# Two transformer blocks on one core: the convolution's splits moved a unit ahead, the entry and the end in another order

## What is computed

```python
def hybrid_mixer(h, ...):
    z = hp @ w_in
    c_q, c_kv, k_pe, gate_b, gate_c, x_in = jnp.split(z, SPLITS, axis=-1)
    ...
    attn = causal_block_attention(q_nope, q_rope, k_nope, k_rope, v)
    u = gate_c * x_in
    u_pad = jnp.pad(u, ((0, 0), (CONV_W - 1, 0), (0, 0)))
    y = sum(conv_w[k] * u_pad[:, k:k + plen] for k in range(CONV_W))
    conv = gate_b * y
    merged = jnp.concatenate([rms_norm(attn[:, PAD_FRONT:], attn_out_norm),
                              rms_norm(conv[:, PAD_FRONT:], conv_out_norm)], axis=-1)
    return merged @ w_out

def second_block(x, ...):
    ...
    h = h + (jax.nn.silu(u @ w_ffn_gate[l]) * (u @ w_ffn_up[l])) @ w_ffn_down[l]
    return rms_norm_2(h, norm_final)
```

## Time and profile before

| | |
|---|---|
| runs shown | 690.18, 691.2, 689.23 us |
| the profiled execution | 689.03 us |
| its span on the core | 687.2 us, so 1.83 us lie around it |
| PE busy | 640.4 us (93%) |
| DVE, ACT, POOL busy | 351.2, 290.0, 51.7 us |
| transferred | 180.73 MB, mean 263 GB/s |

### The profile page before, as it was taken

The page is one execution under the profiler, slowest core; times in us unless marked ns, Lnnn a source line. Parts: engine busy times, 40 slices in busy tenths (PEclk is TensorE's granted clock), DMA queues, the critical chain, the costliest instruction groups (busy, mean ns, idle before and its releaser), DMA issues.

```text
span 687.2 us, 10211 instructions
## 1 busy us (share of the span) xinstructions
PE 640.4 (93%) x4037; PEld 483.7 (70%) x4037; DVE 351.2 (51%) x678; ACT 290.0 (42%) x552; POOL 51.7 (8%) x76
## 2 busy tenths in 40 slices
PE   8999899999999776879899999999999999999995
PEld 5979888842543320424399999998788888888884
DVE  4687664731031020110187766657856666666665
ACT  5855562421011010100182755563665555544554
POOL 3100101100010000000049000000000000000001
PEclk9999999999999997799999999999999999999999
DMA  8956338999999999999997333345535555554101
GB/s 344 419 194 260 116 138 331 403 372 426 427 374 425 420 422 421 422 420 421 422 421 280 123 124 123 123 167 187 185 137 188 189 195 202 198 193 184 62 1 61
DMA packets 26286, 180.73 MB, mean 263 GB/s; under 512 B 3184, under 2 KB 3312, under 8 KB 5120
## 3 DMA queue, kind: packets, MB, share of 16 engines
q1 hardware_dynamic: 25488, 177.89, 65.4%
q10 hardware_dynamic: 752, 2.21, 0.8%
HBM read 179.04 MB, written 1.05 MB: 262 GB/s over the span
## 4 chain that ended last, share of the span: by engine, by line
PE 76%; DMA 11%; DVE 6%; ACT 4%; issue 2%; POOLq 0%; SPq 0%; POOL 0%; ACTq 0%; DVEq 0%
PE ps L1567 73%; DMA ring<-stream_dram 11%; PE ps L1570 3%; DVE ring_r L406 1%; ACT single L399 1%; DVE work L1502 1%; ACT work L850 1%; DVE work L1505 1%; ACT work L757 0%; DVE h L1555 0%; ACT turned L855 0%; ACT work_r L846 0%; DVE work L1388 0%; DVE single L1399 0%; ACT work L764 0%
## 5 line engine op out<-in xcount | busy, mean ns | idle before, releaser
L1567 PE MATMUL ps<-turned,single 128*128 128x256 f32 (+2 forms) x944 | 231.1, 326 | 1.6 <-ACT work L627 0.8
L1567 PE MATMUL ps<-turned,ring_r 128*128 128x256 f32 (+1 forms) x648 | 179.9, 281 | 0.0
L1567 PEld LDWEIGHTS ps<-turned,single 128*128 128x128 f32 x944 | 156.3, 189 | 18.4 <-issue 2.0
L406 DVE TENSOR_TENSOR ring_r<-ring,single 128x1024 fp32r<-128x1024 f32 (+1 forms) x132 | 160.8, 1240 | 14.7 <-ACT single L399 14.7
L399 ACT ACTIVATE single<-ring 128x1024 fp32r<-128x1024 f32 (+1 forms) x132 | 133.8, 1047 | 0.0
L1567 PEld LDWEIGHTS ps<-turned,ring_r 128*128 128x128 f32 x648 | 121.2, 189 | 0.4
L1567 PE MATMUL ps<-ring,work 128*32 128x512 f32 (+2 forms) x462 | 69.8, 612 | 14.7 <-DMA ring<-stream_dram 12.6
L1567 PEld LDWEIGHTS ps<-single 128*128 128x128 f32 x257 | 40.7, 199 | 34.8 <-issue 22.4
L1567 PE MATMUL ps<-work 128*128 128x128 f32 (+5 forms) x310 | 60.5, 378 | 2.6 <-DVE work L1046 1.8
L1567 PE MATMUL ps<-single,turned 128*128 128x512 f32 (+3 forms) x208 | 59.7, 367 | 1.9 <-DVE turned L1187 1.5
L1567 PE MATMUL ps<-single 128*128 128x512 f32 (+1 forms) x257 | 58.0, 367 | 2.9 <-DVE single L1399 1.9
(11 more groups left out here) (254 smaller groups left out, 697.4 us busy)
## 6 DMA issues: line engine op xcount, KB each, us to landing
ring<-stream_dram SPq DMA_DIRECT2D x145, 1024.0 KB, 12.0
work<-stream_dram SPq DMA_DIRECT2D x12, 1024.0 KB, 12.3
turned_w<-stream_dram SPq DMA_DIRECT2D x4, 1024.0 KB, 14.1
extra<-stream_dram SPq DMA_DIRECT2D x2, 1024.0 KB, 9.4
ring<-stream_dram SPq DMA_DIRECT2D x2, 832.0 KB, 7.2
h<-x_dram SPq DMA_DIRECT2D x2, 512.0 KB, 4.5
gain<-gains_dram ACTq DMA_DIRECT2D x2, 512.0 KB, 8.5
yields<-stream_dram SPq DMA_DIRECT2D x1, 1024.0 KB, 12.5
```

Of the source, the lines that this page charges most:

```text
L406: dve.tensor_tensor(ring_r[:, place, a], ring[:, place, a], w_hi[k % HIGHS][:, a].bitcast(F32), ALU.subtract).then_inc(s["wlo_done"], 1)
L1567: return pe.matmul(o, lhsT, rhs, start=start, stop=stop, **kw)
```

## The change

Four things move. At the entry, `vec[:, 0:V_RB]` is issued from ACT's queue, between the meta tokens and the positions, and no longer from SP's; PE's first wait is for constants, meta tokens and the first half of `x` only (`x_in`, 48), and the wait for `vec` and the positions is left to ACT and DVE (`const_in`, 32); the first idle products are three and no longer four, the second two and no longer four. In block 1's attention ACT makes the high parts of rows 0 to 2 in `beside(6)` and of row 3 in `beside(7)`, and the weights' split 10 goes behind these; DVE makes the low parts of rows 0 to 2 in `beside(7)` and of row 3 in `beside(8)`. At the end ACT sums the last squares ahead of `result(0, 1)`; DVE's quarter has a semaphore of its own (`y_left`), for which SP waits; and ACT itself issues the store of the quarter that it finishes last. Two semaphores of extra slots are merged into `const_in`, which then counts 64.

```diff
@@ slot_ready
             elif n == ASIDE_AT + 1 + AGAIN:
-                eng.wait_ge(x_in, 48)
+                eng.wait_ge(x_in, 64)
             elif ASIDE_END - EXTRA <= n < ASIDE_END:
-                eng.wait_ge(extra_full[n - (ASIDE_END - EXTRA)], 16)
+                eng.wait_ge(const_in, 64)
@@ sync
-            sp.dma_start(cst[:, 0:C_FIRST], consts[:, 0:C_FIRST]).then_inc(const_in, 16)
+            sp.dma_start(cst[:, 0:C_FIRST], consts[:, 0:C_FIRST]).then_inc(x_in, 16)
             sp.dma_start(h[:, 0, :], x[0:P, :]).then_inc(x_in, 16)
             sp.dma_start(h[:, 1, :], x[P:TOK, :]).then_inc(x1_in, 16)
-            sp.dma_start(vec[:, 0:V_RB], small[:, 0:V_RB]).then_inc(const_in, 16)
...
-            for i in range(NT):
-                for n in range(2):
-                    sp.wait_ge(s["y_done"], n + 1 if i == 0 else 2 * NT)
-                    sp.dma_start(out[i * P:(i + 1) * P, n * 512:(n + 1) * 512], xn2[:, i, n * 512:(n + 1) * 512]
-                                 ).then_inc(out_st, 16)
+            for n in range(2):
+                sp.wait_ge(s["y_done"], n + 1)
+                sp.dma_start(out[0:P, n * 512:(n + 1) * 512], xn2[:, 0, n * 512:(n + 1) * 512]).then_inc(out_st, 16)
+            sp.wait_ge(s["y_left"], 1)
+            sp.dma_start(out[P:TOK, 512:D], xn2[:, 1, 512:D]).then_inc(out_st, 16)
@@ scalar
             act.dma_start(meta_raw, meta).then_inc(x_in, 16)
+            act.dma_start(vec[:, 0:V_RB], small[:, 0:V_RB]).then_inc(const_in, 16)
             act.dma_start(pos_i[:], positions).then_inc(const_in, 16)
...
-            act.wait_ge(const_in, 48)
+            act.wait_ge(const_in, 32)
...
+            def conv_high(m):
+                act.activation(mrg_hi[:, CT + m, :], mrg[:, m, :], ACT.Copy,
+                               scale=vec[:, V_GCONV + m:V_GCONV + m + 1]).then_inc(s["mrg_high"], 1)
...
                 if u == 6:
+                    act.wait_ge(s["conv_ps"], 3 * CT)
+                    for m in range(CT - 1):
+                        conv_high(m)
+                if u == 7:
+                    conv_square(3)
+                    conv_high(3)
                     split_high_half(act, 10, 0)
-                if u == 7:
-                    act.wait_ge(s["conv_ps"], 3 * CT)
-                    conv_square(3)
-                    for m in range(CT):
-                        act.activation(mrg_hi[:, CT + m, :], mrg[:, m, :], ACT.Copy,
-                                       scale=vec[:, V_GCONV + m:V_GCONV + m + 1]).then_inc(s["mrg_high"], 1)
...
             result(0, 0)
+            last_squares(1, 1)
             result(0, 1)
-            last_squares(1, 1)
             result(1, 0)
+            act.wait_ge(s["y_done"], NT + 1)
+            act.dma_start(out[P:TOK, 0:512], xn2[:, 1, column_half(0)]).then_inc(out_st, 16)
@@ gpsimd
-            pool.wait_ge(const_in, 48)
+            pool.wait_ge(x_in, 48)
@@ vector
-            dve.wait_ge(const_in, 48)
+            dve.wait_ge(const_in, 32)
...
             dve.wait_ge(s["init"], 1)
+            dve.wait_ge(x_in, 48)
...
+            def conv_low(m):
+                dve.wait_ge(s["mrg_high"], m + 1)
+                dve.scalar_tensor_tensor(mrg_lo[:, CT + m, :], mrg[:, m, :], vec[:, V_GCONV + m:V_GCONV + m + 1],
+                                         mrg_hi[:, CT + m, :].bitcast(F32), ALU.mult, ALU.subtract
+                                         ).then_inc(s["convg_done"], 1)
...
                 if u == 7:
                     conv_gated(3)
+                    for m in range(CT - 1):
+                        conv_low(m)
                 if u == 8:
-                    for m in range(CT):
...
+                    conv_low(3)
...
-            dve.tensor_scalar(xn2[:, 1, a], xn2[:, 1, a], rsf[:, 1:2], None, ALU.mult).then_inc(s["y_done"], 1)
+            dve.tensor_scalar(xn2[:, 1, a], xn2[:, 1, a], rsf[:, 1:2], None, ALU.mult).then_inc(s["y_left"], 1)
@@ tensor
-            idle_products(ps[:, 7, 0:ZA], zt[:, 0, 0:P], zt[:, 0, :], 4)
-            pe.wait_ge(const_in, 48)
-            pe.wait_ge(x_in, 32)
+            idle_products(ps[:, 7, 0:ZA], zt[:, 0, 0:P], zt[:, 0, :], 3)
+            pe.wait_ge(x_in, 48)
...
             pe.wait_ge(s["turn_dve"], 1)
-            idle_products(ps[:, 0, 0:ZA], zt[:, 0, 0:P], zt[:, 0, :], 4)
+            idle_products(ps[:, 0, 0:ZA], zt[:, 0, 0:P], zt[:, 0, :], 2)
```

More of the change, by code:

```diff
@@ L311, in two_blocks @@
         full = [sem(f"slot_full{i}") for i in range(SLOTS)]
-        extra_full = [sem(f"extra_full{i}") for i in range(EXTRA)]
         full2 = [sem(f"slot2_full{i}") for i in range(SLOTS)]
@@ L322, in two_blocks @@
             yp_ps yp_sb s2_ps nm2_done e2_done p2_done pt2_ps pt2_sb o2_ps o2_sb sig_done br_ps br_sb
-            mg_done h3_ps h3_done f_ps fsg_done fh_sum fh_high fh_done facc_ps whi_done wlo_done o2_low yp_low mg_sum mg_high att_low cm_ps cm_sb sqs_done h4_done hg_done y_done""".split()
+            mg_done h3_ps h3_done f_ps fsg_done fh_sum fh_high fh_done facc_ps whi_done wlo_done o2_low yp_low mg_sum mg_high att_low cm_ps cm_sb sqs_done h4_done hg_done y_done y_left""".split()
         s = {n: sem(n) for n in names}
@@ L536, in _ @@
                     if n in aside[10:]:
-                        sp.dma_start(home(n), stream[entry_at(n)]).then_inc(extra_full[n - aside[10]], 16)
+                        sp.dma_start(home(n), stream[entry_at(n)]).then_inc(const_in, 16)
                         continue
@@ L594, in _ @@
             split_high(act, 1)
-            act.wait_ge(x_in, 32)
+            act.wait_ge(x_in, 48)
             act.activation(squares_meta, meta_raw, ACT.Square, accum_out=ssx[0:META, 0:1])
@@ L1183, in beside @@
                     conv_gated(3)
+                    for m in range(CT - 1):
+                        conv_low(m)
                 if u == 8:
-                    for m in range(CT):
-                        dve.wait_ge(s["mrg_high"], m + 1)
-                        dve.scalar_tensor_tensor(mrg_lo[:, CT + m, :], mrg[:, m, :], vec[:, V_GCONV + m:V_GCONV + m + 1],
-                                                 mrg_hi[:, CT + m, :].bitcast(F32), ALU.mult, ALU.subtract
-                                                 ).then_inc(s["convg_done"], 1)
+                    conv_low(3)
                 if u in (9, 11, 15):
```

## The result

The changed kernel takes **685.77 us** (median of 15 runs, 684.26 to 688.54) against 689.82 us (median of 15, 688.77 to 691.25) before on the same chip: a ratio of 0.9945, 95% interval 0.9935 to 0.9955, or 4.05 us. The forecast was 685.9 us and 4.0 us. A second measurement of the same changed kernel, beside the last experiments, gave 685.74 us (684.81 to 687.93, 6 runs) against 689.26: 0.9953 (0.9936 to 0.9969).

A forecast was written before the change was run, and what follows sets the result against it. PE was taken to bound the kernel (76% of the chain, transfers 11%). Entry 1.7, attention 1.5 and end 0.8 make 4.0 us off the executions' mean of 689.9: forecast 685.9 us, 8-in-10 range 683.6 to 688.8.

The forecast's parts named there:

- What bounds, and whether early time arrives: Whole kernel: PE holds 76% of the chain; early gain passes whole, since SP issues on PE's release.
- The turns: Entry: with three idle products the turns begin at 6.15 instead of 7.08, 0.93 us sooner.
- The second products and the new wait: Entry: two products, projection at 10.61, then 0.4 us wait for DVE's low half 1; gain 1.7 us.
- The clock: Entry: turns stay at PE's full level, since six records of products still run ahead of them.
- The rival of the late clock: Entry: PE stays at the lower level through the turns, entry loses 1.3 us, 688.9 us in all; chance 0.08.
- The low clock through the projection: Entry: rival with PE at the lower level through the projection, 9.8 us lost, 697.4 us; chance 0.04.
- The attention: Block 1's attention: PE's 1.53 us wait for DVE's first low part goes whole; bounds 1.0 to 1.7.
- The end: After DVE's last sum: squares 0.47 us sooner and one store issue off the path; 0.8 us taken.
- The step on the stores: End: ACT issues its own quarter, so one SP issue of some 0.4 us leaves the path.
- The sum: Whole kernel: 1.7 + 1.5 + 0.8 = 4.0 us off the mean 689.9 gives 685.9 us.

The follow-up runs named there:

- the second profile: Unedited changed kernel, profiled again in its second measurement: median 685.74 us (6 runs) against 689.26 before.
- The first and second term alone: Kernel before with only the entry's part of the change: 688.08 us; with only the attention's part: 688.59 us; before 689.92.
- the three parts alone: Kernel before with one part each: entry 688.08 us, attention 688.59, end 689.29, against 689.92 before.
- the run with one product: Changed kernel with one idle product ahead of the entry's first turns instead of three: 686.08 us, ratio 0.9943 against before.

## Why the prediction was right, step by step

- **What bounds, and whether early time arrives.** Right. SP's eight slots went out 3.51 us sooner, and in the second profile all of the lead was still there at the last sum, over nine profiles all but 0.06 us in mean. The first and second term alone gave 1.84 and 1.33 us.
- **The turns.** Forecast 6.15, read 5.94. The weight load at 6.15 was misread: it is the eighth's, since loads run ahead, but the seventh record starts at 6.15 too, so the number stands. That the turns waited for `vec` was wrong for this profile, though the row names its transfer: the eighth record ran until then, and the wait cost some 0.03 us. What freed the turns here was the product less; in another execution `vec` cost 0.64 us. When the idle products end depends on when the level rises (turns from 5.53 to 6.29 in the profiles with three products), so 5.94 is partly a draw.
- **The second products and the new wait.** Forecast: projection at 10.6, a wait of 0.4 us, the record behind it at 14.2, gain 1.7. Read: 10.55, 0.51, 14.09, 1.82; alone 1.84.
- **The clock.** The turns ran at the full level in the first profile, as I had taken them, but the reason that I gave, six records of products ahead of them, isn't enough: the run without second products has the same six and half-level turns. The rival of the late clock, which I gave 0.08, is an event of single executions and not a case of the kernel. Its price was put too high: 1.3 us lost at the entry instead of 1.7 won are 3.0 apart, and 1.69 were read, since the level was up by the projection. The factor for the half level was too low (1.73 from first products whose row holds the rise at 6.37; the turns give 3.67 / 1.97 = 1.86). The low clock through the projection was seen nowhere: the projection's first twelve records took 2.04 or 2.05 us in both runs with half-level turns.
- **The attention.** Right in mechanism. Forecast 1.53 us whole, with 0.5 us of cover for the scaling; read 1.69 by the lead at 133 us, with 0.58 of cover, and alone 1.72 in its profile, 1.33 by its median. It is more than the wait: the list of waits counts from the modelled end of the products, and a product that need not wait starts ahead of that end (81.44 against 80.51 + 1.29 = 81.80).
- **The end.** The term was mis-sized: 0.8 forecast, 0.68 read, 0.63 alone. The squares gave their 0.47 (0.48 read). The step on the stores counted 0.4 us for an issue that leaves the path by ACT's queue, and the run with SP's store shows that the second queue gave nothing. What else was won at the end, 0.68 - 0.48 = some 0.2 us, came with DVE's quarter no longer waiting for ACT's: by the lines the third store goes out right behind DVE's scaling and no longer behind ACT's. No run has this semaphore alone.
- **The sum.** 4.0 forecast, 4.05 measured, since the entry's and the attention's small surplus met the end's small lack. That it came within 0.05 us is luck: the second measurement gave 3.52, and the three parts alone add up to 3.80. The spread of single runs, of which the half-clock stretch and the late rise (1.7 us each) are two causes, is as large as any one term.

## What to carry over

A gain early in the program arrived at the end here, where the transfers behind it are issued on the engine's release; read who ends the issuing queue's waits before giving the gain up. Put a wait on the engine that uses the data: the first part of `vec` stopped PE, which doesn't read that part. Single profiles here differ by some 2 us for reasons of the clock, so terms of this size are compared by medians, or at a point of the trace ahead of the disturbance.

## What was unexpected of the hardware

- The first rise of TensorE's level falls at different moments of programs that are equal up to there: behind the same three idle products the 16 turns took 1.97 us in one execution (first clock record at 5.53 us) and 3.67 in another (11.45). In the run with one product the level came up at 9.31 us, during a row of turns alone.
- A half-clock stretch from 149 to 152.4 us (granted clock 0.52), behind turns, 4-column products and waits, comes in some executions of a kernel and not in others, and cost 1.7 us there.
- A store of 256 KB from ACT's queue took 2.4 us from issue to landing, SP's of the same size 2.0 to 2.3 us. As the last of the four it landed 0.56 us behind the one ahead of it, issued 0.24 us behind it by ACT or 0.37 by SP, so the longer time need not be the queue's own.
